# Matmul order inside a weight slot, and 32-byte instead of 64-byte places in SBUF, in a three-block model on one core

## The reference

```python
# block 1: SwiGLU feed-forward, RWKV-7 time mix + sliding-window attention, SwiGLU
x = x + 0.5 * swiglu(rms_norm(x), ffn1_gate, ffn1_up, ffn1_down)
p = rms_norm(x) @ w_in                     # 1024 x 2560
x = x + concat(rwkv7(p), attention(p)) @ w_out
x = x + 0.5 * swiglu(rms_norm(x), ffn2_gate, ffn2_up, ffn2_down)
# block 2: recurrent branch and spatial gating, two gated branches, squared-relu MLP
# block 3: S5 + SSD layer, then a retention layer
```

## Time and profile before

| what | value |
|---|---|
| median of 3 runs | 3370.36 us (3368.71 to 3370.56) |
| the profiled execution, its own time | 3370.56 us |
| its span, first to last instruction | 3368.8 us |
| mean granted TensorE clock | 0.914 |
| PE busy | 2927.8 us, 16452 matmuls |
| PE weight loads busy (overlap with PE) | 2381.4 us |
| DVE busy | 1403.9 us |
| POOL busy | 1152.7 us |
| ACT busy | 963.4 us |
| DMA | 251.83 MB, mean 75 GB/s |

### The profile page before, as it was taken

The page is one execution under the profiler, slowest core; times in us unless marked ns, Lnnn a source line. Parts: engine busy times, 40 slices in busy tenths (PEclk is TensorE's granted clock), DMA queues, the critical chain, the costliest instruction groups (busy, mean ns, idle before and its releaser), DMA issues. The chain is left out here.

```text
span 3368.8 us, 39336 instructions
## 1 busy us (share of the span) xinstructions
PE 2927.8 (87%) x16452; PEld 2381.4 (71%) x16452; DVE 1403.9 (42%) x1728; ACT 963.4 (29%) x1282; POOL 1152.7 (34%) x502
## 2 busy tenths in 40 slices
PE   7999999769999999999999989956356698998677
PEld 6888768758888877788888878844225576896455
DVE  4333484444334385442442138346763342003353
ACT  3222331133323244532433222121201322221231
POOL 3444434003444446444444434420000133445012
PEclk9999999869999999999999999977556799999888
DMA  3333220002333222222333333310302223232002
GB/s 136 100 96 103 95 71 22 3 17 88 99 95 105 96 84 79 82 93 92 96 96 97 97 106 95 100 44 6 33 13 37 73 88 100 90 93 69 0 25 75
DMA packets 91463, 251.83 MB, mean 75 GB/s; under 512 B 33440, under 2 KB 34592, under 8 KB 90400
## 3 DMA queue, kind: packets, MB, share of 16 engines
q1 hardware_dynamic: 82080, 247.32, 24.0%
q10 hardware_dynamic: 9216, 2.10, 0.4%
HBM read 240.74 MB, written 6.29 MB: 73 GB/s over the span
## 5 line engine op out<-in xcount | busy, mean ns | idle before, releaser
L438 POOL TENSOR_TENSOR weight_ring_r<-weight_ring,weight_hi_r 128x1024 fp32r<-128x1024 f32 (+2 forms) x412 | 1034.6, 2511 | 1666.0 <-ACT weight_hi_r L431 1666.0
L431 ACT ACTIVATE weight_hi_r<-weight_ring 128x1024 fp32r<-128x1024 f32 (+2 forms) x412 | 448.5, 1089 | 1605.6 <-PE acc L637 1249.4
L637 PE MATMUL acc<-p_r,weight_hi_r 128*128 128x512 f32 x2568 | 770.5, 391 | 19.3 <-POOL weight_ring_r L438 12.7
L637 PE MATMUL acc<-scr_r,weight_hi_r 128*128 128x512 f32 x1888 | 592.3, 395 | 15.6 <-DVE p_r L657 10.4
L637 PEld LDWEIGHTS acc<-p_r,weight_hi_r 128*128 128x128 f32 x2568 | 483.8, 188 | 121.8 <-POOL weight_ring_r L438 19.6
L637 PE MATMUL acc<-p_r,weight_ring_r 128*128 128x512 f32 x1680 | 547.1, 390 | 0.0
L637 PEld LDWEIGHTS acc<-scr_r,weight_hi_r 128*128 128x128 f32 x1888 | 356.1, 189 | 97.0 <-POOL weight_ring_r L438 17.6
L637 PEld LDWEIGHTS acc<-p_r,weight_ring_r 128*128 128x128 f32 x1680 | 316.5, 188 | 66.0
L637 PE MATMUL acc<-h_r,weight_hi_r 128*128 128x512 f32 x952 | 300.2, 397 | 0.1
L637 PE MATMUL acc<-scr_r,weight_ring_r 128*128 128x512 f32 x768 | 237.5, 390 | 0.0
L637 PEld LDWEIGHTS acc<-h_r,weight_hi_r 128*128 128x128 f32 x952 | 180.1, 190 | 45.1 <-issue 7.9
(11 more groups left out here) (518 smaller groups left out, 3753.2 us busy)
## 6 DMA issues: line engine op xcount, KB each, us to landing
weight_ring<-in_weights SPq DMA_DIRECT2D x372, 512.0 KB, 3.5
weight_ring<-in_weights SPq DMA_DIRECT2D x32, 704.0 KB, 4.1
weight_ring<-in_weights SPq DMA_DIRECT2D x8, 640.0 KB, 3.8
x<-in_x SPq DMA_DIRECT2D x4, 512.0 KB, 7.3
lift<-h SPq DMA_DIRECT2D x1, 2048.0 KB, 8.7
p<-lift SPq DMA_DIRECT2D x8, 256.0 KB, 11.3
p<-lift SPq DMA_DIRECT2D x1, 2048.0 KB, 8.8
out<-x SPq DMA_DIRECT2D x1, 2048.0 KB, 7.2
```

The costliest lines, as they stand in the source:

```text
L431: self.nc.scalar.activation(self.r.weight_hi[:, ahead, 0:width], self.weight_ring[:, r, 0:width], ACT.Copy)\
L438: self.nc.gpsimd.tensor_tensor(rest, raw, hi, ALU.subtract).then_inc(self.weights_split, 1)
L637: mm = pe.matmul(product.out(b, m), weights, x_lo if n == 1 else x_hi, start=kx == 0 and n == 0, stop=n == 2 and sub == g.q - 1 and k == g ...
```

## The change

Two edits. In `flow_products` the three loops over k, part n and m become two loops over m and k, with the three matmuls of a pair written next to each other. Within a slot the output chunk m = 0 is finished for all k before m = 1 begins, and neighbouring matmuls write the same bank; before, neighbours wrote the two banks in turn. The wait for an input chunk stands in front of its first use, so in block 0 it is asked for in the m = 0 half only. In `Core.__init__` the arrays behind `weight_hi` come in another order, and places are rounded up to 32 bytes instead of 64.

```diff
             weight_hi=[P, AHEAD, SLOT],
-            scr=[P, 8, T], rstd=[P, T], eye=[P, P], ones=[P, P], small=[P, 256],
+            vec=[P, N_VEC],
             cst=[P, 3980],
-            vec=[P, N_VEC])
-
-        self.r, at = Rounded(), -(-nc.sbuf_base // 64) * 64
+            eye=[P, P], ones=[P, P], rstd=[P, T], scr=[P, 8, T], small=[P, 256])
+
+        self.r, at = Rounded(), -(-nc.sbuf_base // 32) * 32
...
-            at += -(-4 * int(np.prod(shape[1:])) // 64) * 64
+            at += -(-4 * int(np.prod(shape[1:])) // 32) * 32
...
-                for k in range(g.kc):
-                    kx = sub * g.kc + k
-                    if b == 0:
-                        pe.wait_ge(self.input_split, product.inputs + kx + 1)
-                    x_hi, x_lo = op.hi(kx), op.lo(kx)
-                    for n in range(3):
-                        for m in range(g.mb):
-                            w_at = slice(k * g.cols + m * P, k * g.cols + m * P + P)
-                            weights = self.r.weight_ring[:, r, w_at] if n == 2 else self.r.weight_hi[:, ahead, w_at]
-                            mm = pe.matmul(product.out(b, m), weights, x_lo if n == 1 else x_hi, start=kx == 0 and n == 0,
-                                           stop=n == 2 and sub == g.q - 1 and k == g.kc - 1)
+                for m in range(g.mb):
+                    for k in range(g.kc):
+                        kx = sub * g.kc + k
+                        if b == 0 and m == 0:
+                            pe.wait_ge(self.input_split, product.inputs + kx + 1)
+                        w_at = slice(k * g.cols + m * P, k * g.cols + m * P + P)
+                        hi, lo = self.r.weight_hi[:, ahead, w_at], self.r.weight_ring[:, r, w_at]
+                        out = product.out(b, m)
+                        pe.matmul(out, hi, op.hi(kx), start=kx == 0, stop=False)
+                        pe.matmul(out, hi, op.lo(kx), start=False, stop=False)
+                        mm = pe.matmul(out, lo, op.hi(kx), start=False, stop=sub == g.q - 1 and k == g.kc - 1)
                 mm.then_inc(self.products_done, 1)
```

More of the change, by code:

```diff
@@ L347, in __init__ @@
                 alias[name] = Chunks([nc.alloc_sbuf_tensor_at(f"{name}_r{c}", [P, T], F32R, offset=at + 4 * T * c) for c in range(shape[1])])
-            at += -(-4 * int(np.prod(shape[1:])) // 64) * 64
-        self.x, self.h, self.p, self.weight_ring, self.weight_hi, self.scr, self.rstd, self.eye, self.ones, self.small, self.cst, self.vec = place.values()
+            at += -(-4 * int(np.prod(shape[1:])) // 32) * 32
+        self.x, self.h, self.p, self.weight_ring, self.weight_hi, self.vec, self.cst, self.eye, self.ones, self.rstd, self.scr, self.small = place.values()
         self.r.h, self.r.p, self.r.weight_ring, self.r.weight_hi, self.r.cst, self.r.scr = (
```

## The result

The changed kernel takes 3398.9 us (median of 4 runs, 3396.8 to 3402.5); the kernel before, run on the same chip, takes 3370.0 us (4 runs, 3368.7 to 3370.6). The ratio is 1.0088, with a 95% interval of 1.0070 to 1.0105: slower by 29 us. I had predicted 3370.5 us and a range of 3364 to 3381 us, so the time lies outside the range, on the side of rival A.

A forecast was written before the change was run, and what follows sets the result against it. The prediction took TensorE to set the pace in plain matrix-product stages. Its terms, all 0, left the profiled 3370.56 us at 3370.6 us, and 3370.5 us was predicted from the run median, range 3364 to 3381 us.

The forecast's parts named there:

- rival A: Matmuls streaming `scr_r`: a moving operand 32 bytes off costs more, up to 44 us (3415 us); chance 0.07.
- The bound: Plain matrix-product stages: TensorE alone sets the pace, so a change of matmul pitch is paid or gained in full.
- The new order: Reordered matmuls of line 637: no instruction added or removed, pitch and first-block inputs unchanged, 0 us.
- the pitch in the new sequence: 7056 matmuls in eleven products with mb = 2: 0.227 us each before and after, so 0 us.
- the first block's inputs: Block 0 of each product: input chunks asked for sooner, yet splits arrive in time; 0 us, 10 us if uncovered.
- Rival B: First block waits for its inputs: 2.0 us in one product, 10 us in five, 3372.6 to 3381 us; chance 0.02.
- rival C: Neighbouring matmuls with the same weights get cheaper: 32 us saved over 2352 matmuls, 3339 us; chance 0.03.
- The new places: Arrays behind `vec` begin 32 bytes off a multiple of 64: DVE, weight loads and moving operands taken at 0 us.
- the 44 us: Upper bound for the new places: a second fixed part of 0.0135 us on each of 3296 matmuls streaming `scr_r`.

The follow-up runs named there:

- order_only: New matmul loop order on the old SBUF places of the kernel before; 3367.8 us, ratio 1.0003.
- all_off32: Changed kernel with places rounded to 64 bytes and 32 added to the first place, so every array lies 32 off; 3393.9 us, ratio 1.0076.
- seq_round64: Changed kernel with its new array sequence, but places rounded up to 64 bytes instead of 32; 3391.9 us, ratio 1.0075.
- old_scr160: Places of the kernel before, new loop order, `scr` moved up by 160 bytes; 3399.9 us, ratio 1.0091.
- old_weights32: Places of the kernel before, new loop order, `weight_ring` and `weight_hi` moved up by 32 bytes against h, p and scr; 3421.6 us, ratio 1.0157.
- 128 and 192: Places of the kernel before, new loop order, both weight arrays moved up by 128 or 192 bytes; 3418.5 us (1.0147) and 3388.1 us (1.0053).
- old_weights64: Places of the kernel before, new loop order, both weight arrays moved up by 64 bytes; 3424.0 us, ratio 1.0162.

## Why the prediction was wrong

*The bound was right.* PE sets the pace of the flow products and of the retention ones, and a change of its pitch went into the end. By the operand counts of after, 1120 + 768 triples of the flow loop and 320 of line 528 have `scr_r` in them, 3 * 2208 = 6624 matmuls; at 0.232 instead of 0.227 us, more exactly (5.57 - 5.44)/24 = 5.4 ns each, that is 36 us, less 1.7 us (765 * 2.2 ns) in the by-token product. PE's busy time rose by 34.2 us. The span rose by 30.2 us. The 4 us between would be stretches in which PE isn't the bound; I haven't traced them one by one.

*The new order costs 0.* Right, and shown: order_only is at 1.0003. Its parts, the pitch in the new sequence and the first block's inputs, hold as well: 222 matmuls in a window, and the two waits for a split of 10.4 and 6.5 us. (The stretch from 2756.19 us that the earlier trace rows calls `ret_qk` lies in `ab_out`; `ret_qk` starts at 2815.1 us before. The loop and the pitch are the same, 222 matmuls in the window from 2850 us, so the reading stands.) Rival B and rival C fell. One thing the sum couldn't see is that order and place interact: on the displaced `scr` the old order has slots of 5.60 us in `ffn1_up`, the new one of 5.57.

*The new places cost 0.* This is the step that failed. I took 0 "because the two kinds of access that the rows do show, nearest to this one, are not slower". Neither row could show the thing that matters. The weight loads from the odd `cst` mask and the DVE reads tell what a displaced operand costs by itself, and by itself it does cost nothing: all_off32 has every array 32 bytes off and the time of seq_round64. What costs is a distance between arrays, modulo 256: `scr` displaced from the rest cost 29 us in the changed kernel and 32 us in old_scr160, and 256 bytes or a restored multiple of 512 cost nothing. That the distance between the moving operands and the weights loaded beside them is enough for such a loss is shown by old_weights32, 64, 128 and 192 (20 to 55 us). That it makes the changed kernel's 29 us by itself is not shown, and under "Left open" stands what speaks against it. In the kernel before all arrays of the flow products were multiples of 512 apart, so its trace had no displaced pair at all in a stretch where PE set the pace. And nothing in the by-token rows showed that those matmuls could run faster than 0.120 us.

*Rival A* had the right sign, the right operand and a bound that held (up to 3415 us), with a chance of 0.07. Its mechanism, 32 bytes off a boundary of 64, was not the cause. It also put the price on the 3296 matmuls that stream `scr_r`; it falls on their neighbours as well, 5.4 ns a matmul on average. That the measured time lies under rival A's bound is luck and no support for its mechanism.

The rule that I cited beside the sum, 16-byte cachelines of which 32 is a multiple (the Trainium skill, page "SBUF — State Buffer", section Specifications), would have let any such place pass; old_weights32 with 1.0157 shows that for a pair of operands it isn't enough. The same page of the Trainium skill, section "Operand start alignment", says of its own measurements that they are about legality, not speed, and timed nothing; that was the sentence to weigh, and it speaks for a wide bound and not for 0. In the section "🔬 SBUF: two separate sides" this page of the Trainium skill says that "PE, ACT, and DVE's dedicated pair never wait on anyone". That is about other engines, and the trace of old_weights64 agrees as far as it goes: 0.233 us a step under POOL's split and 0.234 without it. But PE's pitch went from 0.2267 to 0.2333 us by moving the weights 64 bytes, which that sentence gives no reason to expect. Whether it is a wait between PE's own two reads or something in how it starts a matmul no run here shows.

The chance was wrong beyond the step. A change whose second half moves one operand of 6624 paced matmuls, on a property of which no row tells, deserved more than 0.07, and a range that took in the 44 us that I had worked out as a bound.

*Left open.* The price isn't one per displaced pair. A matmul that streams `scr` is at the same distance from its weights, modulo 256, whether `scr` is moved up by 64 or the weights by 192. In `ffn1_up` only one matmul in three streams `scr`; with `scr` at 64 the slot is 5.57 us, and with the weights at 192, where all three are displaced, it is only 5.49 us. So the distance to the neighbouring moving operands takes part, or the change of distance from one matmul to the next. Moving operands can't be displaced from each other without displacing one from the weights, and no run separates the two; how the 29 us divide is open. Nor does the price end with the operand. PE in `mlp_down` of after, from the last matmul that streams `scr_r`:

```profile
1880.13 0.39 PE L638 MATMUL acc<-scr_r,weight_ring_r 128*128 128x512 f32 x1
...
1881.76 0.39 PE L636 MATMUL acc<-p_r,weight_hi_r 128*128 128x512 f32 x1
...
1882.89 0.39 PE L638 MATMUL acc<-p_r,weight_ring_r 128*128 128x512 f32 x1
```

The 7 steps up to 1881.76 take 1.63/7 = 0.233 us each although only the first of these matmuls has a displaced operand; the 5 after them take 1.13/5 = 0.226 us. What carries the delay on is open. Distances that aren't a multiple of 32 bytes weren't timed.

## What to carry to other kernels

Where TensorE sets the pace with a weight load for every matmul, the places of the moving operands and of the weights in SBUF belong to the tuning. With 512 moving columns, where the moving operand is the input, keep them a multiple of 256 bytes apart; in the by-token product here the other distances that were timed were the faster ones. After any change of the array list work out the places again: other arrays ahead of `scr` cost about 1% here, and in the sequence rounded to 64 bytes 64 bytes of padding gave it back. Compare the count of matmuls in a full 50 us window in a product that the edit doesn't touch: 217 against 222 there pointed to the layout before any experiment. And when a trace holds no instance of the thing that is changed, near ones that cost nothing give a lower end and not a value.

## What the runs showed of the hardware

- Start to start of fp32r matmuls, 128x128 by 128x512, each with its own weight load, clock at the upper level: 226.7 ns with all moving operands and the weights a multiple of 256 bytes apart; with the weights 32, 64, 128 and 192 bytes further, 233.3, 233.3, 232.4 and 228.9 ns (means over a window of 50 us in `ffn1_up`; the slots are 24 of these, 5.60, 5.60, 5.58 and 5.49 us).
- Adding 32 bytes to all places leaves the time as it was (3391.9 and 3393.9 us); distances between the arrays change it.
- With one matmul in three displaced (`scr` 64 bytes up) the mean step in `ffn1_up` is 232.0 ns; with all three at the same distance from their weights (weights 192 up) it is 228.9 ns.
- In `mlp_down` of after the slower pitch lasts for 7 steps from the start of the last matmul with a displaced operand (0.233 us each, then 0.226 us).
- With 256 moving columns and activations as weights it goes the other way: 0.120 us at a distance of 0, 0.1178 with `scr` (the stationary side) displaced by 160, and 0.1133 with all weights (the moving side) displaced by 192.
